# Gate tiles of block 1 in pairs: seven products in place of eight, the weight sums on GpSimd

## What is computed

```python
gl  = (rmsnorm(x) @ w_in)[..., last 3 * 1024 columns]     # gates, one set for each of 3 branches
pb  = einsum('nbsc,ncd->nbsd', ys, w_branch)              # 3 branches, 512 wide, projected to 1024
merged = einsum('bsnd,nbsd->bsd', sigmoid(gl), pb)
x   = x + merged @ w_out
```

## Time and profile before

| | |
|---|---|
| median of 3 runs | 2316.14 us |
| span of the profiled execution | 2314.2 us |
| TensorE busy | 2303.5 us (100%), 11440 matmuls |
| VectorE busy | 1481.9 us (64%) |
| ScalarE busy | 977.7 us (42%) |
| GpSimd busy | 0.2 us, 4 instructions |
| DMA | 226.78 MB, 98 GB/s on the mean |

### The profile page before, as it was taken

The page is one execution under the profiler, slowest core; times in us unless marked ns, Lnnn a source line. Parts: engine busy times, 40 slices in busy tenths (PEclk is TensorE's granted clock), DMA queues, the critical chain, the costliest instruction groups (busy, mean ns, idle before and its releaser), DMA issues.

```text
span 2314.2 us, 30125 instructions
## 1 busy us (share of the span) xinstructions
PE 2303.5 (100%) x11440; PEld 1881.8 (81%) x11440; DVE 1481.9 (64%) x2785; ACT 977.7 (42%) x1810; POOL 0.2 (0%) x4
## 2 busy tenths in 40 slices
PE   9999999999999999999999999999999999999998
PEld 7888888888888888888877788888887768888887
DVE  6788764345578774344577668566567767668565
ACT  5456542223446553222566533133236664323222
POOL 0000000000000000000000000000000000000000
PEclk9999999999999999999999999999999999999999
DMA  5333343332243333333231132314313113422312
GB/s 175 108 106 105 98 98 113 96 106 86 91 116 105 105 94 117 99 99 110 66 87 55 65 130 91 128 58 143 122 34 97 56 46 101 146 83 91 129 66 98
DMA packets 74766, 226.78 MB, mean 98 GB/s; under 512 B 15296, under 2 KB 16192, under 8 KB 73856
## 3 DMA queue, kind: packets, MB, share of 16 engines
q1 hardware_dynamic: 74480, 224.60, 31.4%
q10 hardware_dynamic: 144, 0.26, 0.0%
HBM read 205.29 MB, written 2.10 MB: 90 GB/s over the span
## 4 chain that ended last, share of the span: by engine, by line
PE 98%; DVE 1%; ACT 0%; DMA 0%; issue 0%; SPq 0%; DVEq 0%
PE bank L591 26%; PE bank L593 26%; PE bank L592 26%; PE bank L2239 2%; PE bank L2238 2%; PE bank L2240 2%; PE bank L1309 2%; PE bank L2055 1%; PE bank L2014 1%; PE bank L1293 1%; PE bank L2039 1%; PE bank L525 1%; PE bank L1282 1%; PE bank L1280 1%; PE bank L2068 1%; PE bank L2097 0%
## 5 line engine op out<-in xcount | busy, mean ns | idle before, releaser
L591 PE MATMUL bank<-h_hi,w_hi 128*128 128x512 f32 x1984 | 785.4, 396 | 0.2
L593 PE MATMUL bank<-h_lo,w_hi 128*128 128x512 f32 x1984 | 774.1, 390 | 0.0
L592 PE MATMUL bank<-h_hi,w_lo 128*128 128x512 f32 x1984 | 773.9, 390 | 0.0
L591 PEld LDWEIGHTS bank<-h_hi,w_hi 128*128 128x128 f32 x1984 | 373.1, 188 | 81.9 <-issue 7.6
L593 PEld LDWEIGHTS bank<-h_lo,w_hi 128*128 128x128 f32 x1984 | 372.7, 188 | 78.7
L1157 DVE TENSOR_TENSOR w_lo<-raw_w,w_hi 128x1024 fp32r<-128x1024 f32 x314 | 379.0, 1222 | 87.9 <-ACT w_hi L1145 84.5
L592 PEld LDWEIGHTS bank<-h_hi,w_lo 128*128 128x128 f32 x1984 | 373.4, 188 | 71.8
L1145 ACT ACTIVATE w_hi<-raw_w 128x1024 fp32r<-128x1024 f32 x313 | 326.7, 1055 | 156.0 <-DMA raw_w<-w_dram 155.6
L2475 ACT ACTIVATE nrm<-bank 128x512 f32<-128x512 f32 x44 | 26.3, 599 | 290.2 <-PE bank L593 290.2
L1609 ACT ACTIVATE ext<-bank 128x512 f32<-128x512 f32 x48 | 28.7, 598 | 275.1 <-PE bank L593 275.1
L1919 DVE TENSOR_TENSOR rope_a<-ext,bank 128x512 f32<-128x512 f32 x32 | 22.0, 688 | 165.8 <-PE bank L593 109.8
(11 more groups left out here) (374 smaller groups left out, 3502.4 us busy)
## 6 DMA issues: line engine op xcount, KB each, us to landing
raw_w<-w_dram SPq DMA_DIRECT2D x312, 512.0 KB, 3.6
down_raw<-w_dram SPq DMA_DIRECT2D x36, 512.0 KB, 4.4
extra_raw<-w_dram SPq DMA_DIRECT2D x10, 512.0 KB, 4.6
k_lo<-k_lo SPq DMA_DIRECT2D x32, 128.0 KB, 2.3
ln_row<-row_dram SPq DMA_DIRECT2D x4, 1024.0 KB, 6.7
last_raw<-w_dram SPq DMA_DIRECT2D x8, 512.0 KB, 4.8
x<-x_dram SPq DMA_DIRECT2D x4, 512.0 KB, 6.4
rowp<-row_dram SPq DMA_DIRECT2D x2, 1024.0 KB, 11.4
```

Of the source, the lines that this page charges most:

```text
L591: nc.tensor.matmul(dst, lh, rh, start=start, stop=False)
L592: nc.tensor.matmul(dst, ll, rh, start=False, stop=False)
L593: return nc.tensor.matmul(dst, lh, rl, start=False, stop=stop)
```

## The change

Feature tiles 0 and 1 stay as they were (`PLAIN_MM = 2`). Tiles 2 to 7 are taken in three pairs, each with its three branches: nine *steps* a layer (`PAIR_STEPS = 9`). In a step the gate product of two feature tiles is a 2 x 2 by 2 x 2 block product: the halves of the 1024 features, the halves of the 512 tokens, and the two feature tiles. It is made by seven block products (4 k-tiles, 256 tokens, three matmuls each) in place of eight. Three of the seven weight blocks are sums of raw weights, which GpSimd forms by four adds of 128 x 512 a step; four of the operand blocks are sums of parts of `h`, which VectorE forms once a layer, into the places of `x` and `rowp`. The products lie in half banks; five pass through two banks that ScalarE copies out between them, and VectorE adds the parts. The projection tiles stay, but their raw weights come through a buffer of their own (`proj_raw`). `x` is read back at the end of the stage (layer 1 writes it to DRAM first), and the loads of `rowp`, `gain_row` and `swa` move behind unit 84.

The core of the diff (in this order: TensorE, GpSimd, ScalarE, VectorE, SyncE):

```diff
+        PAIR_X, PAIR_T, PAIR_R, PAIR_PROJ = T[0], T[1], R, (PT[1], O)
+        PAIR_SEVEN = ((0, PAIR_X), (4, PAIR_T), (5, PAIR_X), (2, PAIR_R), (1, PAIR_X), (6, PAIR_T), (3, PAIR_X))
...
+            def pair_products(s):
+                n, turn = n0 + B1_PAIR + 3 * s, PAIR_STEPS * layer + s
+                for q, (a, bank) in enumerate(PAIR_SEVEN):
+                    if q == 0:
+                        split_wait(pe, n)
+                        if turn:
+                            pe.wait_ge(sig_ready, 2 * turn - 1)
+                    elif q == 1:
+                        pe.wait_ge(sum_split, 2 * turn + 1)
+                        if turn:
+                            pe.wait_ge(product_mixed, 3 * turn)
+                    elif q == 2:
+                        pe.wait_ge(product_copied, 4 * turn + 1)
+                    elif q == 3 and s == 0:
+                        pe.wait_ge(tile_out[0], at(tile_out[0], before1(B1_GATE) + 3 * PLAIN_MM))
+                    elif q == 4:
+                        split_wait(pe, n + 1)
+                        pe.wait_ge(product_copied, 4 * turn + 3)
+                    elif q == 5:
+                        pe.wait_ge(product_copied, 4 * turn + 2)
+                    elif q == 6:
+                        pe.wait_ge(sum_split, 2 * turn + 2)
+                        pe.wait_ge(product_copied, 4 * turn + 4)
+                    if s == 0 and a in COMBO_ORDER:
+                        pe.wait_ge(combo_ready, at(combo_ready, COMBO_ORDER.index(a) + 1))
+                    high, low = pair_weights(n, q)
+                    to = bank[:, FIRST_HALF]
+                    for k in range(4):
+                        w = slice(k * P, (k + 1) * P)
+                        m_hi, m_lo = combo(a, k)
+                        begin = k == 0 and q in (0, 1, 3)
+                        nc.tensor.matmul(to, high[:, w], m_hi, start=begin, stop=False, skip_group_check=True)
+                        nc.tensor.matmul(to, low[:, w], m_hi, start=False, stop=False, skip_group_check=True)
+                        made = nc.tensor.matmul(to, high[:, w], m_lo, start=False, stop=k == 3, skip_group_check=True)
+                    made.then_inc(unit_done if q in (3, 5) else product_done, 1)
...
+            for s in range(PAIR_STEPS):
+                pair_products(s)
+                pair_projects(s)
...
+            def pair_sum(s):
+                for u in (n, n + 1):
+                    pool.wait_ge(raw_loaded[TURN[u] % RAW], 16 * loaded_parts(u))
+                if s:
+                    pool.wait_ge(product_done, 5 * turn - 2)
+                nc.gpsimd.tensor_tensor(sums_raw[:, 0:SEQ], b11, b12, ALU.add).then_inc(pair_sums, 1)
+                pool.wait_ge(pair_sums, 4 * turn + 1)
+                nc.gpsimd.tensor_tensor(b12, b12, b22, ALU.add).then_inc(pair_sums, 1)
+                nc.gpsimd.tensor_tensor(sums_raw[:, SEQ:2 * SEQ], sums_raw[:, 0:SEQ], b22, ALU.add).then_inc(pair_sums, 1)
+            def whole_sum(s):
+                pool.wait_ge(pair_sums, 4 * turn + 3)
+                if s:
+                    pool.wait_ge(product_done, 5 * turn)
+                nc.gpsimd.tensor_tensor(whole_raw[:, :], sums_raw[:, SEQ:2 * SEQ], raw_of(n)[:, SEQ:UNIT], ALU.add).then_inc(pair_sums, 1)
...
                     act.wait_ge(raw_loaded[TURN[u] % RAW], 16 * loaded_parts(u))
+                    if u in STEP_OF and STEP_OF[u][2] == 1:
+                        act.wait_ge(pair_sums, 4 * (PAIR_STEPS * STEP_OF[u][0] + STEP_OF[u][1]) + 2)
                     nc.scalar.activation(hi_of(u), raw_of(u), ACT.Copy).then_inc(hi_cast, 1)
...
+                    elif (mm, i) == (1, 1):
+                        cast_to(act, n0 + B1_PAIR + 1)
+                        sums_high(0)
+                        whole_high(0)
+                        combo_high(4)
+            combo_high(6)
+            act.wait_ge(tile_out[1], at(tile_out[1], before1(B1_GATE) + 3 * PLAIN_MM))
+            for s in range(PAIR_STEPS):
+                product_copy(turn, 1, 1, ext[2][:, FIRST_HALF], PAIR_X)
+                cast_to(act, n + 3)
+                product_copy(turn, 2, 2, ext[3][:, SECOND_HALF], PAIR_T)
+                product_copy(turn, 3, 3, ext[3][:, FIRST_HALF], PAIR_X)
+                proj_high(s)
+                if more:
+                    cast_to(act, n + 4)
+                product_copy(turn, 4, 4, ext[2][:, SECOND_HALF], PAIR_X)
+                if more:
+                    sums_high(s + 1)
+                else:
+                    cast_to(act, n0 + B1_OUT + 1)
...
-            for mm in range(KD):
+            for mm in range(PLAIN_MM):
...
+                    if (mm, i) == (0, 1):
+                        combo_sums()
+                    elif (mm, i) == (1, 0):
+                        combo_low(1)
+                        combo_low(5)
+                    elif (mm, i) == (1, 1):
+                        sums_rest(0)
+                        split_to(dve, n0 + B1_PAIR)
+                        combo_low(4)
+                        split_to(dve, n0 + B1_PAIR + 1)
+                        whole_rest(0)
+                        combo_low(6)
+                merge_out(mm, total)
+            for s in range(PAIR_STEPS):
+                if s:
+                    whole_rest(s)
...
+                proj_rest(s)
...
+                if more:
+                    sums_rest(s + 1)
+                    split_to(dve, n + 3)
+                merge_tile(s, 0)
+                if more:
+                    split_to(dve, n + 4)
+                merge_tile(s, 1)
             split_to(dve, n0 + B1_OUT + 5)
+            dve.wait_ge(x_back, 16 * NB * (layer + 1))
...
+            def load_proj(n):
+                sp.wait_ge(unit_done, n - 2 if STEP_OF[n][1] else n - 4)
+                for unit, c, to, width in pieces(n):
+                    sp.dma_start(proj_raw[:, to:to + width], w_in[unit, :, c:c + width]).then_inc(proj_loaded, 16)
```

More of the change, by code:

```diff
@@ L55 @@
 GATE_TURN = 4
+PLAIN_MM = 2
+B1_PAIR = B1_GATE + 9
+PAIR_STEPS = 9
 B1_OUT = 80
@@ L450, in down_stored, with pair_of, pieces @@
             return first_unit(DEPTH) + layer * B2_STORED + at + 1
+        def pair_of(s):
+            return PLAIN_MM + 2 * (s // 3), s % 3
+        def pieces(n):
+            if n not in STEP_OF:
+                return [(stored_at(n), 0, 0, UNIT)]
+            layer, s, j = STEP_OF[n]
+            m, i = pair_of(s)
+            if j < 2:
+                wanted = [(gate_at(m + j, i), KD)]
+            else:
+                wanted = [(gate_at(m + half, i) + KD, 4) for half in range(2)]
+            out, to = [], 0
+            for first, tiles in wanted:
+                while tiles:
+                    unit, c = divmod(first, KD)
+                    take = min(tiles, KD - c)
+                    out.append((first_unit(layer) + B1_GATE + unit, c * P, to * P, take * P))
+                    first, tiles, to = first + take, tiles - take, to + take
+            return out
         def loaded_parts(n):
-            return sum(2 if m in KR_UNITS else 1 for m in RING[TURN[n] % RAW:TURN[n] + 1:RAW])
+            return sum(2 if m in KR_UNITS else len(pieces(m)) for m in RING[TURN[n] % RAW:TURN[n] + 1:RAW])
         def slot_of(n, ring, extra, last):
@@ L1399, in tensor_block1 @@
             project(0, 2)
-            for mm in range(1, KD):
+            for mm in range(1, PLAIN_MM):
                 for i in range(3):
@@ L1913, in vector_block1, with combo_sums, whole @@
             total, term = ytmp[:, :], rope_a[:, :]
-            for mm in range(KD):
+            def combo_sums():
+                if layer:
+                    dve.wait_ge(x_kept, 16 * NB * layer)
+                raw = [t[:, :, :] for t in combo_raw]
+                def whole(to, k0, cols):
+                    return st(nc.vector.tensor_tensor(to, h_hi[:, k0:k0 + 4, cols].bitcast(F32), h_lo[:, k0:k0 + 4, cols].bitcast(F32), ALU.add))
+                a11 = whole(raw[1], 0, FIRST_HALF)
+                a21 = whole(raw[3], 0, SECOND_HALF)
+                st.wait(whole(raw[5], 4, SECOND_HALF))
+                st.wait(st(nc.vector.tensor_tensor(raw[2], raw[3], raw[5], ALU.subtract)))
+                st(nc.vector.tensor_tensor(raw[5], raw[2], raw[1], ALU.subtract))
+                nc.vector.tensor_tensor(raw[1], raw[1], raw[3], ALU.subtract).then_inc(combo_made, 1)
+                dve.wait_ge(combo_made, at(combo_made, 1))
+                a12 = whole(raw[3], 4, FIRST_HALF)
+                st.wait(a12)
+                nc.vector.tensor_tensor(raw[4], raw[3], raw[5], ALU.add).then_inc(combo_made, 3)
@@ new lines, in whole_rest, with proj_rest @@
+            def whole_rest(s):
+                dve.wait_ge(sum_cast, 2 * (PAIR_STEPS * layer + s) + 2)
+                nc.vector.tensor_tensor(whole_lo[:, :], whole_raw[:, :], whole_hi[:, :].bitcast(F32), ALU.subtract).then_inc(sum_split, 1)
+            def proj_rest(s):
```

(33 more changed lines are left out.)

212 lines of the change are left out of this document (191 added, 21 removed).

## The result

| | before | after |
|---|---|---|
| median | 2315.92 us (4 runs on the same chip) | 2331.68 us (2330.14 to 2332.45, 4 runs) |
| profiled span | 2314.2 us | 2328.3 us |
| ratio, 95% interval | | 1.0067 (1.0053 to 1.0080) |

A forecast was written before the change was run, and what follows sets the result against it. TensorE was taken to bound the kernel, so each matmul removed and each wait counts in full. -15.2 + 8.6 (end) + 6.9 (entry) + 1.4 (product 7) = +1.7 us gave 2318 us, range 2311 to 2330.

The forecast's parts named there:

- The gain: Pair products on TensorE: 84 matmuls of 256 columns replace 48 of 512, saving 0.84 us a pair, 15.2 us in all.
- Rival 5: Seven products don't run at 0.1195 us: a restart at each bank change loses 15 us, 2333 us; chance 0.03.
- The wait before product 7: In each step TensorE waits for ScalarE's fourth copy, behind a cast needing two GpSimd sums: 0.08 us each, 1.4 us.
- The limit T = 1.18 us: T is one GpSimd add, taken as 1.22 us; above 1.18 us product 7 of a step starts late.
- my own chain: From product 3 through two GpSimd adds, cast and copy: 6.12 + 2T, plus 0.12 restart, against product 7's due 8.60.
- rival 1: GpSimd's add paces the step: each 0.1 us past T = 1.18 costs 4.4 us, 2324 at 1.37; chance 0.20.
- Rival 2: GpSimd and VectorE hold each other up after third-branch steps: 0.9 us in four steps, +3.6 us, 2321 to 2322; chance 0.20.
- The end: End of the pair part: output projection's first split comes after both merges, TensorE idle 4.3 us a layer, 8.6 us.
- The entry: Start of the pair part: TensorE waits before products 1 and 3 of the first step, 3.4 us a layer, 6.9 us.
- Rival 3: The clock falls to 1.2 GHz at the end wait, losing 2 us a layer, +4 us, 2322 us; chance 0.04.
- Moved work: Writing and rereading x and later loads of rowp, gain_row and swa: no cost, and no gain from the rowp load.
- The sign: Whether the whole kernel gets slower: chance 0.40 for slower, 0.50 for same, 0.10 for faster.

The follow-up runs named there:

- experiment 6: Kernel after, with GpSimd's third add waiting until VectorE has subtracted the projection's weights: 2332.74 us (one run).
- experiment 9: Kernel after, with ScalarE's fourth copy ahead of the next step's cast and GpSimd's first add of every step made twice: 2332.35 us.
- experiment 10: Kernel with the three reorderings (experiment 4), but VectorE makes all weight sums and GpSimd does nothing: 2301.59 us.
- experiment 2: Kernel after, with VectorE's first split for the output projection put before the last step's two merges: 2317.14 us.
- experiment 3: Kernel after, with VectorE taking plain tile (1,2) before the second split, whole sum's rest and operand 6 at the entry: 2325.86 us.
- experiment 8: Kernel with the three reorderings (experiment 4), but VectorE makes the first step's four weight sums: 2304.20 us.
- experiment 7: Kernel after, with 18 spare matmuls filling TensorE's wait ahead of the output projection: 2326.99 us.
- experiment 5: Kernel after, with GpSimd's first add of every step made twice: 2369.73 us.
- experiment 11: Kernel after in its own orders, but VectorE makes the weight sums and GpSimd does nothing: 2318.82 us.
- experiment 1: Kernel after, with ScalarE making a step's fourth copy before casting the next step's second weight unit: 2323.02 us.
- experiment 4: Kernel after with three reorderings together (fourth copy first, output projection's split before the last merges, entry's late work behind tile (1,2)): 2307.18 us.

## Why the prediction was wrong, point by point

**The gain** was right to the tenth: 84 matmuls of 256 columns at 0.1195 us, seven bank changes without a restart. Rival 5 is out.

**The wait before product 7** was put at 1.4 us and was 6.9: this is the first step that failed. The limit T = 1.18 us held, T did not. GpSimd's add takes 1.30 us and not the 1.22 that I took from VectorE's row for twice the columns, a row that says nothing of GpSimd. At 1.30 my own chain gives 6.12 + 2.60 + 0.12 = 8.84, 0.24 us late; measured was 0.33 in the steps without hold-up, 4.9 us over the 15 steps where it occurs (the last step of a layer has no cast ahead of the copy, which I had counted, and one first step had none). The limit lay so near that 0.08 us on T made the term three times as large. The forecast's own 1.22 lay over the limit already, so by rival 1's own price every further 0.1 us cost 4.4. From the page "GPSIMD Engine Reference" of the Trainium skill (section 3.1: about 2.6 cycles an element for a two-input add, 1.96 times VectorE's time) I had estimated 1.17 us; the trace has 1.30, which is 1.90 times VectorE's 0.684.

**Rival 2, the two engines holding each other up,** was right as a mechanism and in place (0.82 in place of 0.33 after a third branch, 4 x 0.49 = 2.0 us for the 3.6 given; there the first two adds take 1.47 and 1.62 us, 0.49 more together). With it the term is 6.9. It should have been a term of the sum beside rival 1, not a case beside it: both happened. Experiments 6 and 9 show it, as does 10 by its absence. The page "SBUF — State Buffer" of the Trainium skill (section "Who interferes with whom") says that a VectorE instruction with two SBUF inputs contends with a GpSimd one that reads SBUF, and the trace agrees for VectorE's subtractions (0.69 becomes 1.5 to 1.75).

**The end** was forecast at 4.3 us a layer, 4.44 and 4.80 came, released by the split as said. Experiment 2 confirms mechanism and price.

**The entry** was forecast at 3.4 us a layer and was 3.65 and 3.75: the wait before product 1 at 1.45 and 1.65 for 1.2, before product 3 at 2.15 for 2.2. Experiments 3 and 8 each take away the part that they name.

**Rival 3, the clock,** is the second step that failed: the sum had it at nothing, the rival had 4% and a price of 4 us; it happened and cost 4.6, of which 3.0 lie behind the end waits that the rival spoke of and 1.6 at layer 1's entry, where nobody expected it. I had argued from the kernel's end, where the clock held for 4.1 us of idleness, that 4.0 us would just be spared. TensorE was idle for 4.21 and 4.56 us, and the clock fell only 1.04 and 0.57 us behind the restart. A margin of 0.1 us on a single row is no ground for 4%. Experiment 7 shows cause and size for the ends.

**Moved work** cost nothing that shows, as forecast: experiment 10 with the same transfers is 14.5 us under before.

The sum: 5.5 us from the copy's term (3.5 from T and what else its chain took longer, 2.0 from the hold-up), 4.6 from the clock, 1.1 from the end and the entry together and 1.1 from the rest, 12.3 in all; the span moreover lies 3.4 us below the median in place of 1.9. The sign was given 0.40. Each of the rivals 1 to 3 taken as an alternative to the others gave 2321 to 2324; all together, at their own prices (T at 1.30 makes the sum +5.2, then +3.6 and +4), my own sheet gives 2314.2 + 12.8 + 1.9 = 2329.

Why the clock falls behind the entry's waits at one time and not at another stays open. At layer 1's entry it fell in the profiles of after and of experiments 5, 6, 9 and 11, not in those of 1, 2, 3 and 7; at layer 0's in those of 5, 6, 7 and 9 alone. It isn't the kernel by itself, as the two groups of experiment 2's executions show.

## What to carry to other kernels

Work given to an idle engine isn't free even when nobody waits for its result: here GpSimd's adds made VectorE's subtractions up to 2.5 times as long, and the kernels in which VectorE does the adds itself, at 0.69 us each, were 5.6 and 12.9 us faster. When operands are prepared two units ahead, look at the last step of a changed stage, where the preparation for the next stage may have lost its place; one line there was worth 14.5 us. Ahead of an in-order engine's wait for slow work, put whatever frees a bank, and sum the rivals that can happen together.

## What the runs showed of the hardware that I had not expected

- GpSimd's add of 128 x 512 float32 takes 1.30 us, and the next dependent one starts 0.08 us after it. Beside VectorE's two-operand instructions it takes 1.5 to 1.8 in most places, but not in all: the second add of most steps in after stays at 1.29 to 1.30 with 0.96 us of a subtraction beside it, and there VectorE alone is slower.
- The hold-up goes both ways and isn't confined to subtractions: in experiment 4 the cast of `mrg_hi`, one operand, took 1.52 us beside GpSimd in place of 0.43:

```profile
377.21 1.52 DVE L2214 CAST mrg_hi<-ytmp 128x512 fp32r<-128x512 f32 x1
```

- Behind 4.2 to 4.6 us of idle TensorE the granted clock fell to its lower level at both ends in after and in experiments 1, 3, 5, 6, 9 and 11, every kernel with that wait: from 2 us before the restart to 1 us behind it, and then some 8 to 12 matmuls of 512 columns, 3.4 to 5 us, ran at it. Behind the entry's waits (1.4 and 1.9 us close together in after) it fell in some executions and not in others. The single waits of 0.3 to 0.8 us in after's steps never brought it down; those of 2 us in experiment 5 did in several steps.
